# Attention's residual tiles and a reciprocal root in PSUM, and two of ScalarE's steps in another place, in a two-block transformer kernel

## What is computed

```
x = x + g1x * y_x                      # y_x = merged @ w_o, the end of the token mixer
hx2 = _modulate(_rms_norm(x, norm2_g[l]), sh2x, sc2x)
x = x + g2x * _conv_ffn(hx2, rows, ffn_w_up[l], ffn_conv_w[l], ffn_conv_b[l], ffn_w_down[l])
...
# second block, gated delta rule, chunks of 64 in the reference
m = jnp.where(strict, jnp.einsum("bhnid,bhnjd->bhnij", k_beta, k) * decay, 0.0)
a_mat = jnp.eye(CHUNK, dtype=q.dtype) + m
u = lax.linalg.triangular_solve(a_mat, v_beta, left_side=True, lower=True)
```

## Time and profile before

| | |
|---|---|
| median of 3 runs | 1321.68 us (1318.53 to 1322.61) |
| profiled execution, its own time | 1317.53 us |
| its span, first to last instruction | 1315.7 us |
| mean granted TensorE clock | 0.988 |
| TensorE busy | 98% of the span |
| POOL busy | 67% |
| DVE, ACT busy | 55%, 54% |

### The profile page before, as it was taken

One profiled execution on the slowest core, in us unless ns is written; L12 is line 12 of the kernel. 1 busy time (PEld: TensorE's weight loads), 2 busy tenths in 40 slices (PEclk: granted clock), 3 DMA queues, 4 the chain that ended last, 5 costly groups with the idle time before them and its releaser, 6 DMA issues.

```text
span 1315.7 us, 28093 instructions
## 1 busy us (share of the span) xinstructions
PE 1287.7 (98%) x10015; PEld 1219.2 (93%) x10015; DVE 720.4 (55%) x1624; ACT 705.0 (54%) x1250; POOL 875.8 (67%) x383
## 2 busy tenths in 40 slices
PE   9999999999899999999999999999999999999996
PEld 3688899999899999998999989999999999999996
DVE  3989852323886551567354337555633775555623
ACT  3656553554565554475332236666655555666643
POOL 0447965687778879754222217888798787888794
PEclk9999999999999999988998999999999999999998
DMA  9985264355545556633112204555556554655562
GB/s 367 404 317 184 88 218 145 129 175 183 169 144 192 184 160 188 194 106 104 55 59 65 65 33 143 181 183 180 169 163 193 181 177 155 185 181 183 155 191 72
DMA packets 66022, 217.75 MB, mean 166 GB/s; under 512 B 9896, under 2 KB 17320, under 8 KB 62608
## 3 DMA queue, kind: packets, MB, share of 16 engines
q1 hardware_dynamic: 65936, 216.56, 50.7%
HBM read 215.48 MB, written 1.05 MB: 165 GB/s over the span
## 4 chain that ended last, share of the span: by engine, by line
PE 34%; issue 32%; POOL 27%; DVE 4%; ACT 2%; POOLq 1%; ACTq 0%; DVEq 0%
POOL w_lo L598 27%; PE bank L679 11%; PE bank L702 9%; PE bank L1009 5%; PE bank L778 5%; DVE n_lo L2781 1%; ACT w_hi L1538 1%; PE bank L1098 1%; PE bank L1075 1%; DVE bank L2810 0%; DVE cbuf L2839 0%; ACT h L1538 0%; PE bank L1045 0%; POOLq L595 0%; PE bank L1064 0%
## 5 line engine op out<-in xcount | busy, mean ns | idle before, releaser
L598 POOL TENSOR_TENSOR w_lo<-w_raw,w_hi 128x1024 fp32r<-128x1024 f32 x340 | 813.8, 2405 | 398.7 <-ACT w_hi L1538 398.2
L1538 ACT ACTIVATE w_hi<-w_raw 128x1024 fp32r<-128x1024 f32 (+1 forms) x372 | 377.7, 1019 | 138.1 <-PE bank L778 51.3
L702 PE MATMUL bank<-a_hi,w_hi 128*128 128x262 f32 (+2 forms) x1016 | 289.0, 284 | 1.3 <-POOL w_lo L598 1.1
L702 PE MATMUL bank<-a_hi,w_lo 128*128 128x262 f32 (+2 forms) x1016 | 288.5, 284 | 0.0
L702 PE MATMUL bank<-a_lo,w_hi 128*128 128x262 f32 (+2 forms) x1016 | 288.2, 284 | 0.0
L679 PE MATMUL bank<-a_hi,w_hi 128*128 128x256 f32 (+2 forms) x720 | 211.1, 293 | 0.2
L679 PE MATMUL bank<-a_lo,w_hi 128*128 128x256 f32 (+2 forms) x720 | 207.8, 289 | 0.0
L679 PE MATMUL bank<-a_hi,w_lo 128*128 128x256 f32 (+2 forms) x720 | 207.7, 288 | 0.0
L702 PEld LDWEIGHTS bank<-a_hi,w_hi 128*128 128x128 f32 x1016 | 192.7, 190 | 2.0 <-POOL w_lo L598 1.3
L702 PEld LDWEIGHTS bank<-a_lo,w_hi 128*128 128x128 f32 x1016 | 192.8, 190 | 0.1
L702 PEld LDWEIGHTS bank<-a_hi,w_lo 128*128 128x128 f32 x1016 | 192.8, 190 | 0.0
(11 more groups left out here) (485 smaller groups left out, 2566.0 us busy)
## 6 DMA issues: line engine op xcount, KB each, us to landing
w_raw<-in_s SPq DMA_DIRECT2D x284, 512.0 KB, 3.5
w_raw<-in_down SPq DMA_DIRECT2D x48, 512.0 KB, 3.6
adaw<-in_w_ada SPq DMA_DIRECT2D x16, 1024.0 KB, 10.9
w_raw<-in_down SPq DMA_DIRECT2D x24, 384.0 KB, 3.3
adab<-in_w_ada_first SPq DMA_DIRECT2D x8, 1024.0 KB, 8.4
ctxt<-in_ctx SPq DMA_DIRECT2D x1, 1024.0 KB, 11.5
x<-in_x SPq DMA_DIRECT2D x1, 1024.0 KB, 15.5
out_h<-h SPq DMA_DIRECT2D x4, 256.0 KB, 2.7
```

Source lines behind the costliest of these rows:

```text
L598: pool.tensor_tensor(w_lo[:, s], w_raw[:, s], w_hi[:, s].bitcast(F32), ALU.subtract) \
L702: ins = mm(banks[bank][:, tk], w_[:, s, k], x_[:, k, tk], start=(m == 0), stop=(m == 3 * KD - 1))
L1538: return nc.scalar.activation(out_, in_, f, **kw)
```

## The change

Four edits. (1) DVE writes the residual tile to PSUM, `new_x(t)` in bank 5, 6 or 7 by turns, instead of SBUF; ScalarE reads it there for the square and the rounded scaled operand, and copies it to `x` with one further instruction per tile; DVE's `n_lo` reads it there too, and DVE waits for the `n_lo` three tiles back before it writes a bank again. ScalarE's part of this loop is written out instead of `lin`. (2) DVE's reciprocal goes to `r_f`, the other half of bank 5; the eight normalised tiles read it there; a copy to `rstd` comes at k = 7. (3) ScalarE rounds unit 6 of `up0` right after the eight `a_hi` tiles, so ahead of the load of gelu's table, and no longer in `centre(1)`. (4) ScalarE's `flipped("fI2", 2, "tt")` stands two steps ahead, directly behind `product_out(2, 3)`.

```diff
+        def new_x(t):
+            return banks[5 + t % 3][:, 0:N1]
+        r_f = banks[5][:, N1:2 * N1]
...
-            def square_and_scale(t):
-                act.wait_ge(banks_free, t + (TILE0["w_o"] + 5))
-                fn(sq[:, ds(t, 1), 0:N1], x[:, ds(t, 1)], ACT.Square).then_inc(sq_ready, 1)
-                fn(n_hi[:, ds(t, 1), 0:N1], x[:, ds(t, 1)], ACT.Copy, scale=gain[:, 2, ds(t, 1)]).then_inc(split_hi, 1)
-            lin("w_o", None, after=square_and_scale)
+            u0, t0 = UNIT0["w_o"], TILE0["w_o"]
+            for t in range(KD):
+                act.wait_ge(unit_used, u0 + t + 1)
+                round_unit(u0 + t + 4, t % SLOTS)
+                act.wait_ge(banks_free, t0 + t + 5)
+                fn(sq[:, t, 0:N1], new_x(t), ACT.Square).then_inc(sq_ready, 1)
+                fn(x[:, t], new_x(t), ACT.Copy)
+                fn(n_hi[:, t, 0:N1], new_x(t), ACT.Copy, scale=gain[:, 2, t:t + 1]).then_inc(split_hi, 1)
             root(RMS_F, N1, 0)
...
+            act.wait_ge(unit_used, UNIT0["up0"] + 3)
+            round_unit(UNIT0["up0"] + 6, 2)
...
-                    if p:
+                    if p > 1:
                         round_unit(pair * 2 + (u0 + 4), 2 * (p % 2))
...
             flipped("fI1", 1, "tt")
             product_out(2, 3)
+            flipped("fI2", 2, "tt")
             activated(10)
             squared(10)
             tap3(12)
             rounded(12)
-            flipped("fI2", 2, "tt")
...
-                v.scalar_tensor_tensor(n_lo[:, t, 0:N1], x[:, t], gain[:, 2, t:t + 1], n_hi[:, t, 0:N1].bitcast(F32),
+                v.scalar_tensor_tensor(n_lo[:, t, 0:N1], new_x(t), gain[:, 2, t:t + 1], n_hi[:, t, 0:N1].bitcast(F32),
...
-                v.scalar_tensor_tensor(x[:, t], banks[t % SLOTS][:, 0:N1], mod[:, 0, t + 16:t + 17], x[:, t],
+                if t > 2:
+                    dve.wait_ge(split_ready, 8 * S_N + t - 2)
+                v.scalar_tensor_tensor(new_x(t), banks[t % SLOTS][:, 0:N1], mod[:, 0, t + 16:t + 17], x[:, t],
...
-            inverse(RMS_F, N1)
+            dve.wait_ge(split_ready, 8 * S_N + KD)
+            dve.wait_ge(std_ready, RMS_F + 1)
+            link(v.reciprocal(r_f, rstd[:, 0:N1]))
...
-                    v.scalar_tensor_tensor(normed_in(k), x[:, k], gain[:, 2, k:k + 1], rstd[:, 0:N1], ALU.mult, ALU.mult) \
+                    v.scalar_tensor_tensor(normed_in(k), x[:, k], gain[:, 2, k:k + 1], r_f, ALU.mult, ALU.mult) \
                         .then_inc(normed, 1)
+                if k == KD - 1:
+                    v.tensor_copy(rstd[:, 0:N1], r_f)
...
+            dve.wait_ge(split_ready, 8 * S_F + KD)
```

## The result

The changed kernel takes 1309.08 us (median of 5 runs, 1306.86 to 1309.8) against 1319.57 us before (median of 5, 1318.28 to 1322.61); the ratio is 0.9927, 95% interval 0.9907 to 0.9946. Two of the five runs of before are newer than the three that the prediction had.

What follows compares the result with a forecast made beforehand. TensorE is busy 98%, so only its waits or low clock can pay: -1.8 - 1.3 - 0.5 - 0.2 + 1.5 - 5.0 = -7.3, taken as -7.1 from 1321.68, gives 1314.6 us; whole range 1310.0 to 1319.5.

Steps and rivals of the forecast that it cites:

- The five waits: TensorE's waits where the change works, four at the attention/up-projection border, one in the gated delta rule: 6.7 us together.
- Edits 1 and 2: Start of the up-projection: TensorE's waits fall by 1.8 us for `n_lo`, 1.3 for `a_hi`, 0.5 for `a_lo`.
- R: The moment tile 5 of the up-projection begins: 369.11 us before, forecast 365.3, 3.8 us earlier.
- ScalarE's copy: Residual tile loop: ScalarE's work with the added copy takes 2.5 us a tile, covered by TensorE's 2.9 us.
- PSUM's price for DVE: Residual and normalised tiles: reading and writing PSUM priced at nothing, bounds 0 and 0.1 us on the path.
- Edit 3: Up-projection: a loss, tile 8 moves from R + 10.3 to R + 11.8, costing 1.5 us; bounds 0 and +2.3.
- Edit 4: At `y(2,1)` in the gated delta rule: 1.8 us of wait and 3.2 of clock go, 5.0 us gained.
- the base: Time the gain was taken from: profiled execution 1317.53 us, median of the runs 4.15 above it, 1321.68.
- the clock as a term of the sum: Behind the wait before `y(2,1)`: a 1.2 GHz stretch from 618.24 to 625.03 us goes, gaining 3.2 us.
- rival D: Up-projection: edit 3's three waits (0.7, 0.4, 2.0 us) bring the clock down; gain 3.7, 1318.0 us; chance 0.10.
- A: Whole kernel: the main forecast, all edits as priced, 1314.6 us, own range 1311.5 to 1318; chance 0.45.
- rival C: Up-projection: edit 3 costs nothing, ScalarE reaching the table load no earlier relative to R; gain 9.0, 1312.7 us; chance 0.13.

Runs made afterwards that it cites:

- residual_only: Edit 1 alone on the kernel before, with the reciprocal left in SBUF; median 1316.12 us, ratio 0.9978.
- fi2_only: Edit 4 alone on the kernel before; median 1313.50 us, ratio 0.9963.
- before_2 to before_5: The kernel before, unchanged, run four more times for further profiled executions; mean over all 74 executions of that kernel 1318.6 us.
- after_3: The changed kernel, unedited, run for a third profiled execution; mean over all 13 executions of that kernel 1309.6 us.
- after_4: The changed kernel, unedited, run for a fourth profiled execution; mean over all 13 executions of that kernel 1309.6 us.

## Why the prediction was wrong in size

**What bounds the kernel.** Right. The five waits behaved as read, and the lock on two SBUF inputs was shown from both sides, by the whole change and by residual_only. The Trainium skill (SBUF — State Buffer, "Who interferes with whom") states the same rule, that a VectorE instruction with two SBUF inputs contends with a GpSimd instruction that reads SBUF; 2.00 against 0.49 us in residual_only bears it out.

**Edits 1 and 2.** The mechanism was right, and R came 4.1 us earlier where I had 3.8 (364.91 against 369.11, less 0.1 of drift). Without edit 3 tile 8 gains 4.6, since its own small wait of 0.3 and 0.2 of the wait at tile 6 go too. ScalarE's copy (376 ns) was covered. PSUM's price for DVE was 25 ns on the residual that is now written there (469 to 494) and none on the readers.

**Edit 3.** Right, and the sharpest test of the working: R + 11.7 measured, R + 11.8 forecast; without it tile 8 is 1.9 us earlier (forecast 1.5). It is the one part of the change that loses time.

**Edit 4.** Right: 2.0 us of wait and 3.0 us of clock in the traces, in the mean of fi2_only's executions 4.9 for 5.0.

**The steps that failed.** The forecast lies 5.5 us above the measured 1309.08. Two of its steps failed, and the larger is not about the chip.

The first is the base: "The median of the runs is 4.15 us above it, and I expect the same kind of median: 1321.68". That was the median of three executions. The mean of 74 is 1318.6, with a spread of 10.8 us (1312.7 to 1323.5). So 3.1 of the 5.5 us were in the number that the gain was taken from; against 1318.6 the same sum gives 1311.5.

The second is the clock as a term of the sum. I priced one stretch at 1.2 GHz, the one at y(2,1), at 3.2 us and put every other at nothing. The mean time fell by 9.0 us (+-0.6). Tile 8's 2.67 and the 1.97 at y(2,1) make 4.6 of it (I had 3.9), so the clock is worth 4.4. The stretch at y(2,1), which is in all five profiled executions of before, was sized well (3.0 us); the other 1.4 are the term that I had left out. Together: 3.1 from the base, 1.2 from the clock, 0.7 from the starts of tile 8 and y(2,1), and 0.5 because the five executions of the result lie below the mean of the 13, 1309.6. That last part is chance.

Where I went astray on the clock can be named. Against rival D I argued that waits of 1.8, 1.5, 0.5 and 1.1 us "lie within 22 us in the kernel before without a fall". That was true of that execution; the other four of the kernel before that were profiled all have a fall there. So in those the `n_lo` wait cost its 1.8 us and some 1.0 to 1.7 us more: by so much the start of tile 8 stood later in before_2 to before_5. Against that stands edit 3's own fall behind tile 8's wait in two of four executions, which put everything behind it about 1.5 us later in after_3 and after_4. So the net at this place is small as far as these few executions tell.

By place, in profiled executions (five of before, four after), the low time fell from 2.7 to 1.7 us at the up-projection's start, from 6.8 to 0 at y(2,1), from 19.8 to 12.8 elsewhere, and from 7.5 to 5.2 at the program's end. These add up to 17.1 us, but over all timed executions it fell by 11.5 only. So the few profiled executions overstate the difference between the kernels.

Rival D was right as a mechanism: 2 of 4 executions of the changed kernel have a fall behind the waits of edit 3. The Trainium skill (TensorE: Matmul & The Clock Gate, "A second HAM failure mode: psum-queue depth-cycling") says that small idle times between groups of matmuls can make the clock go up and down; these two executions agree. I gave D to the new waits alone, and did not ask the same of the old ones that the change removes.

My range had one fall up or down for A alone, while its lower end made room for none beyond rival C.

**What stays open.** Why there is less of the low clock elsewhere in the delta rule, 7 us in the profiled executions. The change touches nothing there, the numbers scatter from execution to execution, and the kernels with other sets of the edits lie between (13.6 to 20.4 without the wait at y(2,1), 17 to 27 with it). That the place of each sparse stage, moved by 5 us and more, decides it would fit, but was not tested; chance among nine profiled executions is not ruled out either. For all places but y(2,1) together the mean times leave 1.4 us (+-0.6).

## To carry to other kernels

Take the base of a forecast from many executions. Here three of them put it 3 us too high, more than any term of the sum was off.

A short wait of the engine with the gated clock has two prices: its length, and the half speed that may follow. The second is not in every execution, so before a wait is called harmless to the clock, look at several profiled executions, and ask it of the waits that a change removes as well as of those that it adds.

When a step is moved ahead in a strict queue, see what else stood in the idle time that it now sits in front of. Here a 1.28 us table load was pushed out of 2.5 us of idle time for a unit that was needed 0.5 us earlier.

Two inputs in SBUF on VectorE beside a busy GpSimd cost up to 2.2 us (2692 against 473 ns), nearly the whole GpSimd instruction of 2.4; with one of them in PSUM the same tile took 475 ns.

## What the runs showed of the hardware

A wait of TensorE of 1.8 us was enough for the clock to fall to 1.2 GHz behind it: in 5 of 8 profiled executions in dense work, for 3.4 us, and in 9 of 9 in sparse work, for 3.4 or 6.8 us. Matmuls on the identity in the wait at y(2,1) kept it up. The clock also fell, in every kernel, in places where TensorE showed no idle time. TensorE's groups of instructions in the kernel before, from 703.5 us to the fall at 706.95 (busy us, mean ns, idle us before):

```profile
L1246 PE MATMUL bank<-tt,mt 128*128 128x64 f32 x24 | 2.8, 275 | 0.0
L1280 PE MATMUL bank<-tok,sel 8*128 8x256 f32 x4 | 1.3, 438 | 0.0
```

In the 74 executions of the kernel before the time went with the low time: about 0.44 us for each us at 1.2 GHz, with a correlation of 0.94, so most of the scatter of this kernel (0.94 squared is 0.88) goes with the clock.
